# Where the second norm's scale and shift rows are loaded in a one-core decoder layer

## The reference

```python
        x = _layer_norm(DEEPNORM_ALPHA * x + gate1 * mix, ln1_g[l], ln1_b[l])
        h2 = (x * (1.0 + scale2) + shift2).reshape(bsz * seq, d)
        moe = _hierarchical_moe(h2, w_router_group[l], b_router_group[l],
                                w_router_expert[l], b_router_expert[l],
                                w_gate[l], w_up[l], w_down[l]).reshape(bsz, seq, d)
        x = _layer_norm(DEEPNORM_ALPHA * x + gate2 * moe, ln2_g[l], ln2_b[l])
```

## Time and profile before

| | us |
|---|---|
| median of 3 runs | 577.57 |
| lowest, highest | 577.16, 578.74 |
| the profiled execution | 577.13 |
| its span from first to last instruction | 575.3 |

### The profile page before, as it was taken

The page is one execution under the profiler, slowest core; times in us unless marked ns, Lnnn a source line. Parts: engine busy times, 40 slices in busy tenths (PEclk is TensorE's granted clock), DMA queues, the critical chain, the costliest instruction groups (busy, mean ns, idle before and its releaser), DMA issues.

```text
span 575.3 us, 6315 instructions
## 1 busy us (share of the span) xinstructions
PE 512.0 (89%) x2462; PEld 270.8 (47%) x2462; DVE 275.8 (48%) x504; ACT 98.1 (17%) x161; POOL 108.6 (19%) x112
## 2 busy tenths in 40 slices
PE   2999999999999999999956999999998898797762
PEld 1545468644445454445553555555554443443220
DVE  4466999646663753296476232222231221122356
ACT  1000211323132312011032111211111111011000
POOL 2000000244042400076322012211111111000124
PEclk9999999999999999999965999999999988899967
DMA  8999679921322171299299999999999999999473
GB/s 296 355 363 303 218 243 319 305 66 36 129 73 75 12 292 74 89 411 410 109 406 421 370 416 419 414 414 417 416 417 416 417 420 413 417 418 400 180 270 146
DMA packets 68315, 169.47 MB, mean 295 GB/s; under 512 B 7944, under 2 KB 43836, under 8 KB 60092
## 3 DMA queue, kind: packets, MB, share of 16 engines
q1 hardware_dynamic: 62000, 155.37, 70.8%
q0 software_dynamic: 4608, 8.40, 3.9%
q10 hardware_dynamic: 1676, 5.29, 2.3%
HBM read 162.74 MB, written 14.68 MB: 308 GB/s over the span
## 4 chain that ended last, share of the span: by engine, by line
PE 82%; DVE 8%; issue 4%; DMA 4%; ACT 1%; POOL 0%; DVEq 0%; SPq 0%; ACTq 0%; POOLq 0%
PE ps L1441 20%; PE ps L1450 11%; PE ps L1315 11%; PE ps L1362 10%; PE ps L1238 8%; PE ps L1285 5%; PE ps L1432 3%; PE ps L1278 2%; PE ps L1531 2%; PE ps L1304 2%; PE ps L1459 2%; PE ps L1380 2%; DVE acc_rows L827 1%; DMA xg<-h_dram,slot_tok 1%; DVE stay L875 1%
## 5 line engine op out<-in xcount | busy, mean ns | idle before, releaser
L1441 PE MATMUL ps<-w_gu,xT 128*64 128x256 f32 x1024 | 118.8, 385 | 0.0
L1441 PEld LDWEIGHTS ps<-w_gu,xT 128*64 128x64 f32 x1024 | 71.2, 138 | 37.5 <-issue 1.6
L1315 PE MATMUL ps<-hT,w_stage 128*128 128x512 f32 x192 | 84.8, 595 | 0.0
L1450 PE MATMUL ps<-w_dn,hidT 128*64 128x512 f32 x256 | 66.9, 646 | 17.1 <-issue 16.7
L1117 DVE TENSOR_TENSOR ysb<-ps,rows_gate 64x512 f32<-64x512 f32 x64 | 44.1, 689 | 76.9 <-PE ps L1450 76.4
L827 DVE SCALAR_TENSOR_TENSOR acc_rows<-ada_stage,csil,acc_rows 128x256 f32<-128x256 f32 x112 | 55.4, 495 | 4.0
L1362 PE MATMUL ps<-wo,mixT 128*128 128x512 f32 x128 | 55.6, 592 | 0.0
L1315 PEld LDWEIGHTS ps<-hT,w_stage 128*128 128x128 f32 x192 | 35.5, 190 | 41.0 <-issue 41.0
L1108 DVE TENSOR_TENSOR hid<-ps,silu_sb 128x128 f32<-128x128 f32 x32 | 9.3, 292 | 92.0 <-ACT silu_sb L759 92.0
L568 POOL DMA_INDIRECT y_dram<-ysb,slot_row x16 | 16.7, 1042 | 170.5 <-DVE ysb L1117 170.5
L1238 PE MATMUL ps<-hT,w_first 128*128 128x512 f32 x96 | 45.4, 622 | 0.9 <-DVE hT L853 0.9
(11 more groups left out here) (192 smaller groups left out, 486.2 us busy)
## 6 DMA issues: line engine op xcount, KB each, us to landing
w_gu<-in_w_gate_dram SPq DMA_DIRECT2D x32, 1024.0 KB, 20.8
w_gu<-in_w_up_dram SPq DMA_DIRECT2D x32, 1024.0 KB, 23.9
w_dn<-in_w_down_dram SPq DMA_DIRECT2D x32, 1024.0 KB, 24.1
ada_stage<-in_w_ada_dram SPq DMA_DIRECT2D x16, 1024.0 KB, 7.4
w_stage<-in_w_in_dram SPq DMA_DIRECT2D x9, 1024.0 KB, 9.8
ada_in<-in_w_ada_dram SPq DMA_DIRECT2D x16, 512.0 KB, 9.7
wo<-in_w_out_dram SPq DMA_DIRECT2D x1, 4096.0 KB, 14.1
y_tok<-y_dram SPq DMA_DIRECT2D x8, 512.0 KB, 7.4
```

The lines of the kernel that those rows point to most:

```text
L1315: ins = t.matmul(ps[:, 6], st[:, k, (f % 2) * P:(f % 2 + 1) * P], hT[:, k], start=k == 0, stop=k == KC - 1)
L1441: ins = t.matmul(ps[a * SLOTS:(a + 1) * SLOTS, 2 + e, 0:2 * P], rows_in[:, k, e * SLOTS:(e + 1) * SLOTS], weights[:, :, k, a * P:(a + 1) * ...
L1450: ins = t.matmul(ps[b * SLOTS:(b + 1) * SLOTS, 6 + e, :], hidT[e][:, a * SLOTS:(a + 1) * SLOTS], weights[:, a, b * 512:(b + 1) * 512], sta ...
```

## The change

The loads of `g2r` and `bb2r` move from their place ahead of SP's wait for the last scatters to a place among the reloads, behind the two of tile 0 and ahead of the six others. DVE's wait for them moves from ahead of the tile-0 sum to ahead of `centre(0)`, the first instruction that reads g2r. Nothing is added, removed or resized.

```diff
@@ SP
             for i in (3, 1, 2, 0):
                 sp.dma_start(x1_back[:, i], x1_dram.rearrange("(i p) n -> i p n", p=P)[i]).then_inc(ld_x1[i], 16)
-            sp.dma_start(g2r[:], ln2_g[0].partition_broadcast(P)).then_inc(ld_g2, 16)
-            sp.dma_start(bb2r[:], ln2_b[0].partition_broadcast(P)).then_inc(ld_g2, 16)
             for n in range(Y_RING):
                 sp.wait_ge(scattered[n], 16 * (NPAIR // Y_RING))
             for i in range(TC):
                 for k in range(2):
                     sp.dma_start(y_tok[i][:, k], y_dram.rearrange("(i p k) n -> i k p n", p=P, k=2)[i, k]
                                  ).then_inc(ld_y[i][k], 16)
+                if i == 0:
+                    sp.dma_start(g2r[:], ln2_g[0].partition_broadcast(P)).then_inc(ld_g2, 16)
+                    sp.dma_start(bb2r[:], ln2_b[0].partition_broadcast(P)).then_inc(ld_g2, 16)
@@ DVE
-            dve.wait_ge(ld_g2, 32)
             dve.wait_ge(ld_x1[0], 16)
             for k in range(2):
                 dve.wait_ge(ld_y[0][k], 16)
                 link(w.scalar_tensor_tensor(out=x1_back[:, 0], in0=y_tok[0][:, k], scalar=wk[:, k, 0:1],
                                             in1=x1_back[:, 0], op0=ALU.mult, op1=ALU.add))
             statistics(0, x1_back[:, 0])
+            dve.wait_ge(ld_g2, 32)
             centre(0, x1_back[:, 0])
```

## The result

| | before | after |
|---|---|---|
| median, us | 577.96 (5 runs) | 580.99 (5 runs) |
| lowest, highest | 577.16, 578.74 | 580.06, 581.64 |
| profiled execution, us (span) | 577.13 (575.3) | 581.28 (579.5) |

The changed kernel is slower: the ratio is 1.0047, with an interval from 1.0033 to 1.0060, so +2.7 us (+1.9 to +3.5). The prediction was 579.1 us, +1.5, just inside "no difference", with 0.38 for slower. It was made on a median of 577.57; the ratio carried to that gives 580.3, inside the range up to 580.8. The bare median, 580.99, is 0.2 above the range, and the median of before went up by 0.4 with its two further runs.

A forecast was written before the change was run, and what follows sets the result against it. The prediction took the kernel's end to hang on the last scatter and then tile 1's first reload, which starts PE at L1531. Terms -1.1, +2.6 and 0 gave +1.5 us on 577.57: 579.1 us, range 577.2 to 580.8.

The forecast's parts named there:

- What bounds the kernel: Last 55 us: last scatter, then tile 1's first reload, set PE's start at L1531; the end shifts one to one.
- Part 1: Ahead of the last scatter: without the two loads one late DMA engine frees earlier, scatter lands in 3.4 us; gain 1.1 us.
- The first rival: At the scatter nothing is gained, the loads cost 2.6 to 3.3 us among the reloads: 580.2 to 580.9 us; chance 0.20.
- The sentence from the Trainium skill on turns between queues: At the scatter: engines alternate queues by packet group, so it waits only for one group; gain could not reach 2.5 us.
- Part 2: Among the reloads: the two loads delay the third reload, tile 1's first, by 2.6 us, bounds 2.5 and 3.3.
- The other price: Among the reloads: their landings give 1.39 us for each load, 2.8 us for two.
- The estimate by the Trainium skill's fixed cost: Among the reloads: a fixed 2.0 us per DMA, paid one after another, would add 4 us to the 2.6.
- Part 3: DVE's moved wait at centre(0): already met by 0.6 us, over 5 us of lateness covered; effect nothing.
- The sum: PE's start at L1531: -1.1 + 2.6 = +1.5 us, carried to the median 577.57, gives 579.1 us, 0.26% slower.
- The clock rival: PE's clock after restart rises at the same moment, half of 1.5 us returns: 578.3; chance 0.15 with the later-engine rival.
- a sign of being wrong: Stretch from PE's start at L1531 to the end, 24.3 us, changing by more than 1 us.
- The other two rivals: At the scatter, a later engine gains 2.5 us: 577.7, 0.15 with the clock's; or unforeseen, faster by over 0.3%: 0.05.

The follow-up runs named there:

- e3: Kernel before without the loads of g2r and bb2r; GpSimd fills their tiles with ones behind the last scatter; ratio 1.0009 to the kernel before.
- e9: Kernel before with two more 512 KB broadcast rows ahead of g2r and bb2r, so four ahead of the last scatter; ratio 1.0019 to the kernel before.
- e12: Changed kernel with 10 useless matmuls (fillers) on PE while it stands for the reloads; ratio 1.0005 to the kernel before.
- e6: Changed kernel with g2r and bb2r filled from 128 different rows each of x1_dram, not one row read 128 times; ratio 1.0027 to the kernel before.
- e5: Changed kernel with two more 512 KB broadcast rows right behind g2r and bb2r among the reloads; ratio 1.0102 to the kernel before.
- e1: Kernel before with only DVE's wait for g2r and bb2r moved ahead of centre(0), SP's order unchanged; ratio 0.9994 to the kernel before.
- e7: Kernel before with 8 useless matmuls (fillers) on PE ahead of its wait for the reloads; ratio 0.9956 to the kernel before.
- e11: Kernel before with 7 useless matmuls (fillers) on PE ahead of its wait for the reloads; ratio 0.9961 to the kernel before.

## Why the prediction was right in its range and too low

- **What bounds the kernel**: right. The chain went through the same scatter and the same reload, and the 10.7 us behind PE's last row did not move.
- **Part 1 (-1.1)**: the step that failed for the median. The mechanism is right: without the two loads the late engine is done 19.4 us after g_back, which in the first profile would have been 540.0, as the prediction had it. A scatter that the engine does not hold lands in 3.58 us and not in 3.4, so in that execution the gain would have been 0.9. But it was sized on one execution and carried to the median, and that execution was of the rarer kind, with the last experts at the full clock and the scatter at 19.0 us. In the others the late engine is done first and the gain is 0: `e3` has 1.0009 without the two loads. The forecast assumed, with no row for it, that a stage of one execution is that of the median. The first rival said just this ("in most executions no engine is behind when the scatter comes"), and at 580.2 to 580.9 it was the nearest to what was measured.
- The sentence from the Trainium skill on turns between queues (DMA: Bandwidth & Descriptors, "Queues, rings and completion order") was read as a bound: the scatter would wait only for the group under way. `e9` does not bear this reading out as a small bound: with two rows more ahead the scatter landed 2.1 us later, with its last 7 packets behind all that SP's queue had left. How large a group is, the traces do not show.
- **Part 2 (+2.6)**: the term was mis-sized. It measured +3.1 in the profiles (9.98 against 6.87; 10.09 in `e12`), inside its bounds of 2.5 to 3.3. The choice of the cheap end rested on the broadcast's source, and `e6` shows no such advantage. The other price, twice the 1.39 us between landings, would have been 2.8. With more rows (`e5`) each costs 1.7. SP's issues were hidden, as worked out: 0.43 and 0.44 us.
- The estimate by the Trainium skill's fixed cost (DMA: Bandwidth & Descriptors, "Anatomy of one DMA"), 4 us more, was rightly left aside. That section gives the 2.0 us for a DMA issued from GpSimd, and these two are SP's; they cost 3.1 us together in a running train.
- **Part 3 (0)**: right. `e1` has 0.9994, and in the changed kernel bb2r landed 0.6 us ahead of centre(0), the margin that the prediction gave.
- **The sum**: with part 1 at 0 and part 2 at 3.1 it gives +3.1 us, 577.96 + 3.1 = 581.1; measured were +2.7 by the ratio and 580.99 as the median. Both terms were off in the same direction, by 1.1 and 0.5. The range held the result because it was drawn for just this case, no gain and dear loads.
- **The clock rival**: not as put. The granted clock was back at 557.2 in the first profile of before, and in the changed kernel soon after 560. That is 6.1 us after PE's restart in the one and 3.7 in the other: neither the same moment nor the same distance, the two cases that the rival weighed. In the profiles of this case PE's 24 rows take from 11.9 to 13.6 us with the idle stretch ahead of them, in the kernel before 13.59 and 12.65. Two executions of one kernel differ by 0.9 us here, so the -1.23 between the two first profiles says nothing on the change. By it the stretch from PE's start to the end went from 24.3 to 23.1 us, more than the 1 us that the prediction named as a sign of being wrong, though it had excepted the clock. `e7` against `e12` shows that the loss is the same with the clock kept up, as far as their intervals go.
- **The other two rivals** fell. A later engine does hold the scatter longer (`e9`), but no profile of the kernel before has one, and nothing made it faster.
- The difference was called "no difference" with 0.57; it was slower by more than 0.3%, which had 0.38. Had part 1 been sized for the usual execution and not for the profiled one, the forecast would have been slower, the case of the first rival.

The fillers alone make the kernel before faster: `e7` at 0.9956 and `e11` at 0.9961 beat both kernels, with the loads where they were.

## What to carry to other kernels

A load ahead of a wait is free while the wait ends later anyway; put among the transfers that an engine stands for, it costs its whole transfer (here 1.55 us for 512 KB), so ask first which reload the chain waits for and move only behind that one. A gain read from one profile at a place where two things meet (here a late DMA engine and a scatter) holds only for executions that meet the same way: look at what sets the time of arrival, and take a second profile of the same kernel before carrying it to the median.

## What was unexpected of the hardware

- The same kernel issued its last scatter 19.0 us after g_back in one execution and 21.9 in another, with a granted clock of 1.00 and 0.50 in the window from 529 to 533. Over fourteen profiles the mean granted clock between the two issues (1.00, 0.92, 0.84) goes with the time between them (19.0, 20.4 to 20.7, 21.9).
- Some DMA engines are behind the others at the end of a train of eight 512 KB loads, at last a single one. It is done 22 us after the train's first issue in both profiles of the kernel before (542.56 less 520.62, and by 542.3 less 520.28), while the share of the 16 has fallen to 0.28 already in the window from 537 to 539. With six loads it is done at 19.4, with ten at 24.5: some 1.27 us for each load. Why this engine is behind, no run shows.
- A scatter that met this engine was delayed by all that SP's queue still had on it: 0.89 us late with 0.85 us of SP's packets left, 2.1 with 2.0.
- Filling 6 to 7 us of PE's idle time with useless matmuls took 2 to 3 us off its next 24 rows (10.5 and 10.6 against 12.65 and 13.59), and 2.3 to 2.5 us off the kernel.
